# Expert layers: one gather of 8 KB rows per slot becomes a gather of key rows and a gather of value rows, each with its own wait

## The reference

```
q    = x @ w_q                            # 8 heads, two halves of 128
s    = q . sub_keys                       # 128 scores for each half
idx  = top 16 of the sums of the two top-16 lists      # for each row and head
gate = softmax of those 16 sums
h    = x . u_tab[idx]                     # one dot product per retrieved key row
out  = sum over 8*16 of gelu(h) * gate * v_tab[idx]
```

## Time and profile before

| | us |
|---|---|
| median of 3 runs | 4558.36 |
| runs | 4556.71 to 4558.56 |
| the profiled execution's own time | 4570.19 |
| its span, first to last instruction | 4568.4 |

### The profile page before, as it was taken

The page is one execution under the profiler, slowest core; times in us unless marked ns, Lnnn a source line. Parts: engine busy times, 40 slices in busy tenths (PEclk is TensorE's granted clock), DMA queues, the critical chain, the costliest instruction groups (busy, mean ns, idle before and its releaser), DMA issues. The chain is left out here.

```text
span 4568.4 us, 45641 instructions
## 1 busy us (share of the span) xinstructions
PE 3653.2 (80%) x13271; PEld 1977.5 (43%) x13271; DVE 2677.0 (59%) x6397; ACT 951.9 (21%) x2394; POOL 1396.5 (31%) x1188
## 2 busy tenths in 40 slices
PE   7977878787787887887778778778787787887777
PEld 6866765333333333333333456533333333333332
DVE  3423451577777677776624433227777777677783
ACT  2212321221212212121112322112121212212120
POOL 0002330243444434444400010004444444444442
PEclk8987989899998999999879888889998998999987
DMA  2221001699999999999921043329999999999996
GB/s 89 73 58 38 3 1 38 257 380 368 393 372 385 381 373 395 382 362 384 392 81 54 0 158 146 121 80 385 389 376 372 390 374 384 373 371 395 364 389 244
DMA packets 200759, 1207.43 MB, mean 264 GB/s; under 512 B 28936, under 2 KB 48656, under 8 KB 65056
## 3 DMA queue, kind: packets, MB, share of 16 engines
q0 software_dynamic: 152448, 1133.58, 62.3%
q1 hardware_dynamic: 48160, 72.24, 4.7%
HBM read 1197.88 MB, written 7.86 MB: 264 GB/s over the span
## 5 line engine op out<-in xcount | busy, mean ns | idle before, releaser
L1172 PE MATMUL po<-ring,diag 128*128 128x512 f32 x4096 | 2045.4, 654 | 579.5 <-ACT diag L1037 577.0
L994 POOL DMA_INDIRECT ring<-in_uv,idx x1024 | 1224.8, 1196 | 1944.3 <-PE po L1172 1462.4
L1083 DVE SCALAR_TENSOR_TENSOR ring<-ring,xn 128x1024 f32<-128x1024 f32 x1024 | 1224.8, 1223 | 534.8 <-DMA ring<-in_uv,idx 499.5
L1172 PEld LDWEIGHTS po<-ring,diag 128*128 128x128 f32 x4096 | 826.1, 209 | 1626.4 <-issue 972.3
L1032 ACT ACTIVATE hg<-hs 128x4 f32<-128x4 f32 x256 | 52.6, 205 | 2002.6 <-DVE ring L1083 2002.6
L1037 ACT ACTIVATE diag<-gated,hg 128x128 f32<-128x128 f32 x1024 | 327.1, 390 | 15.6 <-ACT hg L1032 8.9
L1132 PE MATMUL pq<-xnT,w 128*128 128x512 f32 (+1 forms) x512 | 261.6, 596 | 1.5 <-ACT q L1012 1.5
L269 PE MATMUL acc<-xnT,w 128*128 128x260 f32 x1024 | 229.3, 386 | 5.1 <-ACT inp L305 4.2
L269 PEld LDWEIGHTS acc<-xnT,w 128*128 128x128 f32 x1024 | 195.9, 192 | 38.2 <-ACT inp L305 6.6
L1133 PEld LDWEIGHTS pqs<-xnT,w 128*128 128x128 f32 x512 | 97.8, 191 | 116.7 <-issue 108.2
L1059 DVE TENSOR_TENSOR gated<-const,gate 128x2048 f32<-128x2048 f32 x64 | 146.7, 2293 | 2.2
(11 more groups left out here) (441 smaller groups left out, 4090.9 us busy)
## 6 DMA issues: line engine op xcount, KB each, us to landing
w<-in_w_gdn SPq DMA_DIRECT2D x32, 512.0 KB, 3.6
w<-in_w_peer SPq DMA_DIRECT2D x32, 512.0 KB
ring<-in_uv,idx POOLq DMA_INDIRECT x1024, 9.8
S<-in_state_ssm SPq DMA_DIRECT2D x16, 256.0 KB, 2.9
out_ssm_s<-S SPq DMA_DIRECT2D x16, 256.0 KB, 3.1
w<-in_w_gdn_out SPq DMA_DIRECT2D x2, 2048.0 KB
w<-in_w_mla_out SPq DMA_DIRECT2D x2, 2048.0 KB
wq<-in_w_uq SPq DMA_DIRECT2D x1, 3072.0 KB
```

The lines of the kernel that those rows point to most:

```text
L994: pool.indirect_dma_start(out=ring[:, c % RING, :], out_offset=None, in_=uv, in_offset=bass.IndirectOffsetOnAxis(ap=idx[t % 2][:, c:c + 1] ...
L1083: dve.scalar_tensor_tensor(ring[:, c % RING, 0:D], ring[:, c % RING, 0:D], 1.0, xn[:, t, :], ALU.mult, ALU.mult, accum_out=hs[a][:, c:c + ...
L1172: last = pe.matmul(po[a][:, HALF * e:HALF * e + HALF], diag[:, c % RING, :], ring[:, c % RING, D + HALF * e:D + HALF * e + HALF], start=c ...
```

## The change

The table `uv` is split into `u` and `v`, rows of 4 KB. Each slot is filled by two indirect DMAs from POOL: one of 128 key rows into the first half of the place, which waits for the dot product of slot c-8, and one of 128 value rows into the second half, which waits for TensorE's use of slot c-8. Both read the same column of indices. They stand on POOL's queue in the order key of c, value of c, key of c+1, value of c+1. DVE waits for `landed`, which the key DMA now counts up; PE waits for the diagonal and for `valued`, which the value DMA counts up. ACT waits for `pv` ahead of each group of four diagonals, where before it did so at slots 0 and 8. The sample rows' 8 slots are filled by pairs too.

```diff
+                def fetch(r, e, numbers):
+                    pool.indirect_dma_start(out=ring[:, r, D * e:D * e + D], out_offset=None, in_=tables[e],
+                                            in_offset=bass.IndirectOffsetOnAxis(ap=numbers, axis=0)).then_inc(s[f"{('landed', 'valued')[e]}{r}"], 16)
+
...
                         for c in range(TOPK):
                             if c >= RING or t or not first:
+                                apart(pool, at("dot", u, c - RING + 1))
+                            fetch(c % RING, 0, idx[t % 2][:, c:c + 1])
+                            if c >= RING or t or not first:
                                 apart(pool, at("pv", u, c - RING + 1))
-                            pool.indirect_dma_start(out=ring[:, c % RING, :], out_offset=None, in_=uv,
-                                                    in_offset=bass.IndirectOffsetOnAxis(ap=idx[t % 2][:, c:c + 1], axis=0)).then_inc(s[f"landed{c % RING}"], 16)
+                            fetch(c % RING, 1, idx[t % 2][:, c:c + 1])
...
                     pool.wait_ge(s["pv"], UNITS * TOPK - RING + j + 1)
-                    pool.indirect_dma_start(out=ring[:, j, :], out_offset=None, in_=uv,
-                                            in_offset=bass.IndirectOffsetOnAxis(ap=sidxT[:, j:j + 1], axis=0)).then_inc(s[f"landed{j}"], 16)
+                    for e in range(2):
+                        fetch(j, e, sidxT[:, j:j + 1])
...
-                                if c == RING or c == 0:
-                                    after(act, at("pv", u, c - RING + GRP_C) if c or t or not first else (s["pv"], 0))
+                                if c % GRP_C == 0 and (c >= RING or t or not first):
+                                    after(act, at("pv", u, c - RING + GRP_C))
...
-                            after(pe, at("diag", u, c + 1))
+                            after(pe, at("diag", u, c + 1), at(f"valued{c % RING}", u, 16 * (c // RING + 1)))
...
+                for b in range(NS):
+                    pe.wait_ge(s[f"valued{b}"], 32 * UNITS + 16)
...
-        **{f"uv{l}": np.concatenate([x["peer_u"][l], x["peer_v"][l]], 1) for l in range(2)},
+        **{f"{n}{l}": c(x[f"peer_{n}"][l]) for n in "uv" for l in range(2)},
```

More of the change, by code:

```diff
@@ L920, in top_k, with peer @@
     assert done[0] == TOP_STEPS, done[0]
-def peer(core, xn, xns, xnT, weight, keys, uv):
+def peer(core, xn, xns, xnT, weight, keys, tables):
     nc = core.nc
@@ L935, in peer @@
                flipped=2, rowed=1, sdot=1, sgelu=1, sact=2, spv=1, sadded=1,
-               **{f"landed{r}": 32 for r in range(RING)}) as s, ExitStack() as ctx:
+               **{f"{n}{r}": 32 for r in range(RING) for n in ("landed", "valued")}) as s, ExitStack() as ctx:
         at = s.at
@@ L2019, in peer_layer @@
         norm(core, core.i["norm_ffn"][layer:layer + 1, :], xn, xns, xnT)
-        peer(core, xn, xns, xnT, core.i[f"w_peer{layer}"], core.i[f"keys{layer}"], core.i[f"uv{layer}"])
+        peer(core, xn, xns, xnT, core.i[f"w_peer{layer}"], core.i[f"keys{layer}"], (core.i[f"u{layer}"], core.i[f"v{layer}"]))
 def program(nc, ins, outs):
```

## The result

| | before | after |
|---|---|---|
| median of runs, us | 4558.46 | 4733.80 |
| runs, us | 4556.71 to 4568.49 | 4729.31 to 4744.28 |
| span of the profiled execution, us | 4568.4 | 4730.0 |

The changed kernel is slower: ratio 1.0386, 95% interval 1.0365 to 1.0408. I had said 4905 us, in a range of 4640 to 5110. The direction and the engine were right; the loss is 175 us, half of the 347 forecast.

What follows compares the result with a forecast made beforehand. It took a loop around eight places as the bound, with POOL having room. Split, POOL's issues at 1.56 us would bind: 3192 against 2843 us, so 4558.4 + 349 = 4907, said as 4905, range 4640 to 5110 us.

Steps and rivals of the forecast that it cites:

- POOL becomes the bound: Gathers in both layers: POOL without pauses at 1.56 us an issue, 3192 us against 2843, +349 us.
- the hold: POOL's issue starting under a DVE instruction with two SBUF inputs stands still until that ends, then needs 0.81 us.
- An issue costs the same whatever it moves: POOL's indirect DMAs: about 0.94 us whatever the row bytes, 1.24 us back to back, so halving rows halves nothing.
- 8.8 us a unit from dots: POOL beside dot products: nearly every dot catches an issue and holds it 0.55 us, by 16 a unit.
- the spreading: DVE's spreading of gates (2293 ns) catches one POOL issue a unit and holds it, say, 1.7 us.
- Today's mean: Lower price for a POOL issue: the kernel before's 1196 + 300 ns, 1.496 us, with POOL resting half the time.
- Ends of a layer: 0: Sample pairs some 6 us slower, last gathers landing sooner: taken as 0, with 6 us a layer each way.
- The order on the queue is worth 0: POOL's queue: keys come at most one slot earlier; with POOL slowest, waits are nearly always fulfilled, worth 0.
- Transfers: DMA queues: 4 KB packets at 172 ns, 4% dearer, up to 0.11 us a slot, hidden under POOL, charged nothing.
- PE's wait for `valued`: PE's product: value asked for 1.56 us behind its key; hidden, if not at most 6 us a unit.
- ACT's for `pv`: ACT before each four diagonals waits for products two groups back: 0; if binding, it would hold PE, not POOL.
- Rival D: Each POOL issue takes the shared ports from DVE for 0.94 us: +1120 us, 5680 us; chance 2%.

Runs made afterwards that it cites:

- e4: Changed kernel with the dot products' second input a constant row in PSUM: 4783.4 us, ratio 1.0501 to the kernel before.
- e1: Changed kernel with key and value gathers both waiting for TensorE's use of slot c-8: 4803.4 us, ratio 1.0548 to the kernel before.
- e13: Changed kernel with all slots split, but ordered four keys then four values: 4602.8 us, ratio 1.0105 to the kernel before.
- e7: Kernel before with dot products over 64 of 1024 numbers: 4387.4 us, ratio 0.9623 to the kernel before.
- e8: Changed kernel with dot products over 64 of 1024 numbers: 4434.6 us, ratio 0.9722 to the kernel before.
- e12: Three of each four slots split, three keys then three values, the fourth from the joint table: 4566.6 us, ratio 1.0026 to the kernel before.
- e2: Kernel before plus one gather of 128 rows of 16 bytes behind each slot's gather: 4789.3 us, ratio 1.0522 to the kernel before.

## Why the prediction was right in direction, and where its size went

- **POOL becomes the bound: right**, in that it idles only its 0.30 us gaps and the gathers' length grew by 174.5 us. But it is not the only bound near: without the hold POOL has pauses and the kernel is 1.1% slower still (e4). A faster issuer alone would not have saved this change. Of the signs named, POOL's mean (1.17 us, said 1.2 to 1.3) and the rate (359 GB/s, said 340) came out on the mild side, as the hold did.
- **An issue costs the same whatever it moves: right**, down to 16 bytes a row (1191 ns). The back-to-back period of 1.24 us held too.
- **The hold, the step that was mis-sized.** The prediction had 1.56 us an issue, of it 0.32 of hold; it came to 1.475, 0.235 of hold. Its working was 8.8 us a unit from dots, 1.7 from the spreading, 0.4 from small ones, 10.9 in all; measured are 32 x 0.235 = 7.5. Counted from 1000 to 2300 us of the changed kernel, the term that failed is the one for dots: 374 issues start under 439 dots, so nearly every dot does catch one, as said, but together they lose 161 us, 0.37 us a dot where 0.55 was charged; that is 5.9 us a unit. The spreading took 1.2 and the small ones 0.25. The wrong premise is that an issue under a dot loses half of it on average, and in a dense train 1.05 us for every two dots. Many fall nearly in step with the dots and lose under 0.1 us (153 of the 374). Today's mean (1.496), which I gave as the lower end, was the better guide, and slightly above the truth. The reason given for leaving it was wrong: the share of issues that start under a dot was 45% before (210 of 464) and 42% after (374 of 881). 2 x 1023 x (1.56 - 1.475) = 174 us, against a miss of 171.
- **"Ends of a layer: 0": somewhat too high.** The stretches after a layer's last gather became 9.3 and 8.7 us shorter.
- **"The order on the queue is worth 0": wrong.** With both halves late the ratio is 1.0548, with keys first 1.0105, for the same number of issues. Taking out the early key makes POOL wait for places (e1); putting keys first shortens its issues (e13).
- **Transfers: right.** 175 ns for 4 KB against 172 taken. Their price was hidden under POOL's; where dots are short the split costs at most 2.3% of the rate (e7, e8).
- **PE's wait for `valued` and ACT's for `pv`: no cost seen** in the changed kernel: POOL, which sets the time, hardly ever waits for PE. With keys first PE's wait shows (248 us), at no cost that a run has measured.
- **Rival D, the hold on DVE: nothing of it is seen.** The longest dot of the changed kernel's middle took 1297 ns, and the dot at 1537.89 starts 0.26 us into an issue and takes its usual 1.23 us. The Trainium skill (SBUF — State Buffer, "SBUF: two separate sides") says that whoever starts first has the shared ports for the whole instruction. That is what POOL's copy does to DVE here (1554 ns a dot against 1223); for an indirect DMA's issue ahead of DVE this trace does not agree. With keys first the dots stand 1.27 us apart instead of 1.15; whether the issues keep them off or the landings pace them is open.

What stays open: which wait of the loop holds the changed kernel without the hold (e4), with dots at 1217 ns; and how much of e12's time is the loop's.

## What to carry to other kernels

Count indirect DMAs, not bytes: each costs its issuing engine some 1.24 us however small its rows, and more beside VectorE instructions with two SBUF inputs. To split a transfer for the sake of one early half can pay where the issuer would be waiting anyway (here 0.4% with half of the slots split) and loses once the issuer has no pauses left. Look for the bound by gaps of one engine that are all alike, not by the DMA share, which stood at 0.96 on either side of the change. An engine without pauses is not by that the only bound: here, with its issues made shorter and nothing else relieved, the time did not fall (e4).

## What the runs showed of the hardware

- Issue of an indirect DMA of 128 rows, where DVE does not hold it: 0.94 to 0.95 us for rows of 16 B (median of all, e2) to 32 KB, plus 0.30 us until the next.
- An issue that starts under a DVE instruction with two SBUF inputs ends 0.79 to 0.83 us behind that instruction's end in three cases of four (changed kernel, 1000 to 2300 us). With one of the inputs in PSUM the dots do not hold it (mean 988 ns; the spreading still does, the issue at 1515.80 of e4 taking 2.25 us).
- Beside a GpSimd memset, which reads nothing, a small TENSOR_SCALAR of DVE took 1080 ns instead of 165 (medians), but dots, with two SBUF inputs, stayed at 1228 ns.
- With two or three of four slots split, single issues took up to 6.1 and 6.2 us; the longest in the changed kernel was 2.8. The cause was not looked for.
